# Up projection of a gated feed-forward block: eight half-size products per tile replaced by Strassen's seven, from the fourth tile on

## The reference

```
x = layer_norm(ALPHA * x + mix, ln1_g, ln1_b)            # 1024 prompt rows and 32 sample rows, 1024 columns
up = x @ ffn_w_up                                        # 1024 x 5632
u_conv, u_lin = up[..., :D_FF], up[..., D_FF:]           # D_FF = 2816
conv = sum(padded[:, j:j + T] * ffn_conv_w[j] for j in range(3)) + ffn_conv_b
h = silu(conv) * u_lin
x = layer_norm(ALPHA * x + h @ ffn_w_down, ln2_g, ln2_b)
```

## Time and profile before

| | |
|---|---|
| median of 3 runs | 1707.56 us |
| profiled execution | 1713.04 us, span 1711.3 us |
| TensorE busy over the span | 1600.2 us (94%) |
| VectorE, ScalarE, GpSimd busy | 929.2, 665.8, 337.5 us (54, 39, 20%) |
| rest of tile 0 to tile 21 of the up projection | 1002 to 1461 us |
| down projection | 1461 to 1703 us |
| granted TensorE clock | 1.00 from 897 us on, mean of the span 0.955 |

### The profile page before, as it was taken

How to read it: one execution, slowest core, us unless ns; L and a number is a source line. 1 busy time by engine, 2 the same in 40 slices (tenths; PEclk the granted TensorE clock), 3 DMA queues, 4 the chain that set the end, 5 groups by cost and what they waited for, 6 DMA issues and landing times.

```text
span 1711.3 us, 39992 instructions
## 1 busy us (share of the span) xinstructions
PE 1600.2 (94%) x17211; PEld 1160.9 (68%) x17211; DVE 929.2 (54%) x2152; ACT 665.8 (39%) x1145; POOL 337.5 (20%) x209
## 2 busy tenths in 40 slices
PE   6899999979899788988879999999999999999998
PEld 4486666645667566766658866666666666888887
DVE  3699999985767557777532954333333333000046
ACT  4733222114677545666463143333333333211110
POOL 3322111012210211121113022222222222111100
PEclk9999999988999788899889999999999999999999
DMA  8123121333511203010122212111111110511001
GB/s 298 47 75 125 51 92 52 101 134 118 180 53 29 60 18 111 23 41 3 53 112 79 112 65 75 50 50 50 50 50 50 50 50 30 200 50 51 26 26 77
DMA packets 50370, 126.85 MB, mean 74 GB/s; under 512 B 17426, under 2 KB 24338, under 8 KB 42354
## 3 DMA queue, kind: packets, MB, share of 16 engines
q1 hardware_dynamic: 49106, 123.23, 21.2%
q0 software_dynamic: 1088, 1.05, 0.2%
HBM read 100.49 MB, written 23.77 MB: 73 GB/s over the span
## 4 chain that ended last, share of the span: by engine, by line
PE 70%; DVE 21%; ACT 4%; issue 3%; SPq 2%; DMA 1%; DVEq 0%; ACTq 0%
PE bank L2294 66%; DVE arena L2698 12%; PE bank L2457 2%; DVE arena L2718 1%; PE bank L1031 1%; PE bank L976 1%; DVE arena L2734 1%; DVE arena L2658 1%; SPq L924 1%; DVE arena L2716 1%; DVE arena L2719 1%; ACT L1405 1%; DVE arena L1648 0%; DVE arena L2712 0%; PE bank L1911 0%
## 5 line engine op out<-in xcount | busy, mean ns | idle before, releaser
L2294 PE MATMUL bank<-arena 64*64 64x64 f32 (+11 forms) x16504 | 1515.9, 288 | 91.7 <-ACT arena L1378 17.7
L2294 PEld LDWEIGHTS bank<-arena 128*128 128x128 f16 (+7 forms) x16504 | 1083.5, 123 | 523.1 <-issue 133.3
L2810 POOL TENSOR_TENSOR arena<-arena 128x2048 f16<-128x2048 f32 x53 | 216.0, 4078 | 775.0 <-ACT arena L2500 762.5
L2698 DVE TENSOR_SCALAR_CACHE_REDUCE arena<-arena 128x384 bf16<-128x384 f32 (+6 forms) x231 | 196.9, 917 | 1.2
L2499 ACT ACTIVATE arena<-arena 128x2048 f16<-128x2048 f32 x53 | 100.7, 1901 | 167.2 <-PE bank L2294 144.0
L2098 DVE TENSOR_SCALAR arena<-arena 128x1072 f32<-128x1072 f32 x22 | 26.5, 1205 | 172.7 <-issue 165.6
L2516 ACT ACTIVATE arena<-bank 128x352 f32<-128x352 f32 x72 | 33.2, 463 | 189.0 <-PE bank L2294 189.0
L1782 POOL TENSOR_TENSOR arena<-arena 128x512 f32<-128x512 f32 x40 | 54.7, 1377 | 258.4 <-PE bank L2294 127.7
L2500 ACT ACTIVATE arena<-arena 128x2048 f32<-128x2048 f32 x53 | 100.5, 1896 | 0.0
L2110 DVE SCALAR_TENSOR_TENSOR arena<-bank,arena 128x352 f32<-128x352 f32 (+1 forms) x66 | 33.5, 513 | 111.3 <-PE bank L2294 84.5
L2837 POOL TENSOR_TENSOR arena<-arena 128x512 f32<-128x512 f32 (+1 forms) x32 | 38.5, 1206 | 199.6 <-DVE arena L2767 116.0
(11 more groups left out here) (265 smaller groups left out, 1137.7 us busy)
## 6 DMA issues: line engine op xcount, KB each, us to landing
arena<-slabs SPq DMA_DIRECT2D x53, 1024.0 KB, 5.0
arena<-kcache SPq DMA_DIRECT2D x32, 256.0 KB, 2.9
arena<-vcache SPq DMA_DIRECT2D x32, 256.0 KB, 3.1
prw<-arena SPq DMA_DIRECT2D x42, 176.0 KB, 1.9
arena<-xt SPq DMA_DIRECT2D x4, 1056.0 KB, 8.4
x1d<-arena SPq DMA_DIRECT2D x8, 512.0 KB, 2.6
arena<-x1d SPq DMA_DIRECT2D x1, 4096.0 KB, 13.1
y<-arena SPq DMA_DIRECT2D x8, 512.0 KB, 2.6
```

The lines of the kernel that those rows point to most:

```text
L2294: return nc.tensor.matmul(out, lhsT, rhs, start=start, stop=stop, skip_group_check=True)
L2698: last = dve.tensor_scalar(junk, a, s, None, op, ALU.add, accum_out=cnt[:, k:k + 1])
L2810: pool.tensor_tensor(WL[r].rearrange("p a b -> p (a b)"), STG[s], WH[r].rearrange("p a b -> p (a b)"), ALU.subtract).then_inc(slab_lo, 1)
```

## The change

Tiles 0 to 2 are computed as before. From tile 3 on (`UP_PLAIN` = 3) the product of a tile's weights and the activations is taken as a 2 x 2 block product: the weights in blocks (convolved or linear half; blocks 0 to 3 or 4 to 7 of the model columns), the activations in blocks (model columns; first or second half of the tokens, 528 each, `TH2`). The seven products of Strassen's method (in Winograd's form) are made instead of eight, each over 4 column blocks. `UP_PRODUCTS` gives their order, the bank pair of each and the moving operand. A product is two jobs of 12 matmuls of 264 columns (`TC`). The banks a, d and c take a first product, which ScalarE copies out, and then go on accumulating a second one on top; b takes one. Eight banks in all, a pair for each letter; a job waits for the same bank of the tile before.

- Token sums: VectorE makes T1, T2, T4 and GpSimd T3 (`TF`, sums and differences of quarters of XH and XL, 4 x 528 = 2112 elements a partition, five and three instructions), ScalarE writes their high parts (`TH`), VectorE three low parts and GpSimd one (`THL`). This is done once, in tiles 0 to 2.
- Weight sums, every tile from 3 on: ScalarE scales the slab (`up_scale`), VectorE makes four sums of 4 x 128 elements (`up_sums`), ScalarE writes 7 x 512 high parts in four instructions (`up_hi`) and GpSimd the low parts in four (`up_lo`).
- Results, every tile from 3 on: ScalarE copies six half banks into `UQ1`, `UQ7`, `UQ5` and the final a pair into `HF`. VectorE combines b, d and c with them, and builds the fourth block from SBUF alone. Convolution, SiLU, h and its two parts are as before, but h of tile f is made while tile f+1 runs, and its product is SBUF by SBUF.
- h of tiles 8 to 18 is written to DRAM (`hd`, 11 x 540 KB), each before a later slab is loaded, and read back when the up projection ends, into the place of the token sums and of `UQ`, `US`. TensorE waits for the reads before the second and third slab group of down (n = 0).
- The fourth weight slab of down is loaded after the up projection instead of in it; the conv output is stored later.

```
+UP_PRODUCTS = (("a", "x11"), ("d", "t3"), ("c", "t1"), ("b", "t2"), ("a", "x21"), ("d", "t4"), ("c", "x22"))
+UP_BANKS = (("b", "dve"), ("a", "act"), ("d", "dve"), ("c", "dve"))
...
+            def up_products(f):                      # TensorE
+                i = f - UP_PLAIN
+                wh, wl = UWH[f % 2], UWL[f % 2]
+                for c, (name, rhs) in enumerate(UP_PRODUCTS):
+                    xh, xl, k0, t0 = moving[rhs]
+                    if c in (0, 2, 4):
+                        pe.wait_ge(uw_lo, 3 * i + c // 2 + 1)
+                    if c == 6:
+                        pe.wait_ge(slab_lo, SL_UP + f + 1)
...
+                    for n in range(2):
+                        if c < 4:
+                            b = open_bank(pe, (name + "up", f, n))
+                        else:
+                            b = bank((name + "up", f, n))
+                            pe.wait_ge(part_read, 6 * i + 2 * (c - 4) + n + 1)
+                        s = slice(t0 + TC * n, t0 + TC * n + TC)
+                        for k in range(4):
+                            w = slice(up_weight(c, k), up_weight(c, k) + P)
+                            mm(b[:, 0:TC], wh[:, w], xh[:, k0 + k, s], c < 4 and k == 0, False)
+                            mm(b[:, 0:TC], wh[:, w], xl[:, k0 + k, s], False, False)
+                            last = mm(b[:, 0:TC], wl[:, w], xh[:, k0 + k, s], False, k == 3)
+                        last.then_inc(part_filled if c < 3 else filled, 1)
...
             for n in range(3):                       # down, TensorE
...
                     if n == 0:
                         pe.wait_ge(hl_ready, sum(DN_G[:g]) + kn)
+                        for q in ((), (0, 1), (2,))[g]:
+                            pe.wait_ge(h_in[q], 16)
...
+            for f in range(UP_PLAIN, FT):            # ScalarE
+                i = f - UP_PLAIN
+                if i:
+                    act.wait_ge(q_ready, 2 * i)
+                for k, (name, dst) in enumerate((("a", UQ1), ("d", UQ7), ("c", UQ5))):
+                    if i and k == 1:
+                        act.wait_ge(c22_ready, i)
+                    for n in range(2):
+                        act.wait_ge(part_filled, 6 * i + 2 * k + n + 1)
+                        act.activation(dst[:, TC * n:TC * n + TC], bank((name + "up", f, n))[:, 0:TC], ACT.Copy,
+                                       scale=UN).then_inc(part_read, 1)
+                if f + 2 < FT:
+                    up_scale(f + 2)
+                if i:
+                    up_silu(f - 1)
+                act.wait_ge(hl_ready, f - 1)
+                for n in range(2):
+                    b = wait_job(act, ("aup", f, n))
+                    act.activation(HF[:, f % 2, TC * n:TC * n + TC], b[:, 0:TC], ACT.Copy, scale=UN).then_inc(freed["act"], 1)
+                if i:
+                    up_hh(f - 1)
+                if f + 2 < FT:
+                    up_hi(f + 2)
...
             for f in range(UP_PLAIN):                # ScalarE, tiles 0 to 2; m = 0 banks, then:
+                if f == 0:
+                    token_hi(0)
+                    token_hi(1)
+                    token_hi(2)
+                if f == 2:
+                    token_hi(3)
...
+                up_silu(f)
                 act.activation(HH[f], HF[:, f % 2, :], ACT.Copy, scale=XS).then_inc(hh_ready, 1)
+                if f == 0:
+                    up_scale(UP_PLAIN)
+                if f == 1:
+                    up_hi(UP_PLAIN)
+                    up_scale(UP_PLAIN + 1)
+                if f == 2:
+                    up_hi(UP_PLAIN + 1)
...
+            token_sum(0, ...)                        # VectorE, ahead of tile 0: three instructions of 2112
+            token_sum(1, ...)                        # two
             for f in range(UP_PLAIN):                # VectorE, after conv, h and the low part of tile f:
+                if f == 0:
+                    token_lo(0, 0, 1)
+                    up_sums(UP_PLAIN)
+                if f == 1:
+                    token_lo(1, 1, 2)
+                    dve.wait_ge(t_lo, 2)
+                    token_sum(0, ...)                # two
+                    token_lo(3, 0, 3)
+                    up_sums(UP_PLAIN + 1)
...
+            for f in range(UP_PLAIN, FT):            # VectorE
+                i, u = f - UP_PLAIN, UPB[:, f % 2, :]
+                dve.wait_ge(cn_ready, f - 1)
+                dve.tensor_copy(sampled_up(u, 0, 2), SCV[:, f, :].rearrange("p (b x) -> p b x", x=2))
...
+                    b = wait_job(dve, ("bup", f, n))                         # twice
+                    dve.scalar_tensor_tensor(UQ[:, s], b[:, 0:TC], UN, UQ1[:, s], ALU.mult, ALU.add).then_inc(freed["dve"], 1)
...
+                link(dve.scalar_tensor_tensor(UQ5, UQ5, 1.0, UQ, ALU.mult, ALU.add))
+                dve.scalar_tensor_tensor(u[:, 2 + TH2:2 + T], UQ5[:, 0:pn], 1.0, UQ7[:, 0:pn], ALU.mult, ALU.add)
...
+                if i:
+                    up_h(f - 1)                                              # 1024 and 32 elements
+                if f + 2 < FT:
+                    up_sums(f + 2)                                           # four of 512
+                for n in range(2):
+                    b = wait_job(dve, ("dup", f, n))
...
+                if i:
+                    up_hl(f - 1)
+                for n in range(2):
+                    b = wait_job(dve, ("cup", f, n))
...
+                up_conv(f)
...
+            pool_link(pool.tensor_tensor(TF[2], quarter(XH, 1, 1), quarter(XH, 0, 1), ALU.subtract))   # GpSimd, once
+            pool_link(pool.tensor_tensor(TF[2], TF[2], quarter(XL, 1, 1), ALU.add))
+            pool.tensor_tensor(TF[2], TF[2], quarter(XL, 0, 1), ALU.subtract).then_inc(t3f_ready, 1)
+            def up_lo(f):
+                for g, (c0, c1) in enumerate(UP_GROUPS):                     # 1024, 1024, 1024, 512 elements
...
+                    pool.tensor_tensor(UWL[f % 2][:, s], up_source(f, g), UWH[f % 2][:, s],
+                                       ALU.subtract).then_inc(uw_lo if g < 3 else slab_lo, 1)
...
+                if f == 0:                                                   # GpSimd, per tile, after the CN copies
+                    pool.wait_ge(t3_hi, 1)
+                    pool.tensor_tensor(THL[2], TF[2], TH[2], ALU.subtract).then_inc(t3_lo, 1)
+                if 0 < f < FT - 2:
+                    up_lo(f + 2)
...
+            for w in range(SL_UP + 4, SL_DN + 3):                            # SyncE
+                f = w - SL_UP - 5
+                if 0 <= f - HKEEP < HSPILL:
+                    sp.wait_ge(hl_ready, f + 1)
+                    sp.dma_start(hd[f - HKEEP], arena[:, HB[f]:HB[f] + TOK]).then_inc(h_out, 16)
                 load_slab(w)
...
             sp.wait_ge(filled, plan.last_of_slab[SL_DN - 1] + 1)
+            sp.wait_ge(h_out, 16 * HSPILL)
+            reload(0, 0, 5, MX0)
+            load_slab(SL_DN + 3)
+            reload(1, 5, 3, MX0 + 5 * TOK)
+            sp.wait_ge(hl_ready, FT)
+            reload(2, 8, HSPILL - 8, UP0)
```

235 lines of the change are left out of this document (194 added, 41 removed).

## The result

| | before | after |
|---|---|---|
| median, of 4 runs each | 1708.14 us | 1686.14 us |
| lowest to highest | 1707.27 to 1714.22 | 1685.49 to 1691.91 |
| profiled execution, span | 1713.04, 1711.3 us | 1686.14, 1684.4 us |
| TensorE waits of tiles 0 to 4 | 0 | 22.99 us |
| TensorE's restart to the start of down | 458.34 us | 435.85 us |

The ratio is 0.9866, 95% interval 0.9845 to 0.9887: 22 us faster. Predicted were 17 us (1691): 49 us of TensorE's own time, less what the start of the new scheme, the lower clock after its waits and VectorE's loop in the steady state were to cost.

A forecast was written before the change was run, and what follows sets the result against it. TensorE alone was taken to bound both projections. 1713.0 (profiled execution) - 49.0 + 25.5 + 2.5 + 4 + 0 = 1696.0, less 5.5 to the median: 1690.5, said as 1691 us; range 1667 to 1714, the forecast's own 1681 to 1701.

The forecast's parts named there:

- TensorE's own time: 19 changed tiles of the up projection: each from 21.48 to 18.90 us, 49.0 us saved in all.
- Turns of VectorE and GpSimd: Changed tiles: VectorE instructions with two SBUF sources and GpSimd's block each other; 6.4 us a tile, less 0.15 to 0.2 for each of five.
- VectorE's loop, 19.1: Steady state: VectorE's loop of 19.1 us against TensorE's 18.9 sets the tile; 4 us of TensorE waiting over 17 tiles.
- Start of the scheme, 25.5: Tiles 0 to 3: token and weight sums make TensorE wait 4.8, 3.9 and 16.8 us, 25.5 us in sum.
- Lower clock after waits, 2.5: After TensorE's waits the granted clock stays lower for a while: 2.5 us lost, bounds 0 and 6.
- Start of down, 0: Start of down: split and read-back done at +17.5 us, hidden behind 21.7 us of TensorE work; cost 0.
- 5.5 us between the profiled execution and the median: Whole kernel: the median shown is 5.5 us below the profiled execution, so 1696.0 becomes 1690.5.
- A: Changed tiles: holding does not bite, pieces fall into VectorE's idle time, the start costs 8 us; 1667 us; chance 0.13.
- B: Changed tiles: held instructions save nothing of their own time, loop 20.4 us; about 1711 us; chance 0.17.
- C: Changed tiles: VectorE and GpSimd in series set the tile, 21.2 us; slower, 1726 us; chance 0.12.
- D: Start of down: waits for the read-back, 5 us and a clock fall of 2; 1698 us; chance within the forecast's 0.58.

The follow-up runs named there:

- the kernel with one more pass: Against the kernel after: a second convolution pass (two SBUF sources, 1072 columns) made twice on VectorE in each changed tile; stretch 439.40 us, median 1691.44 us.
- the kernel with half a last product: Against the kernel after: the seventh product of each changed tile over two of its four blocks; stretch 417.63 us, median 1666.04 us.

## Why the prediction was right, point by point

The costs against the 49 us were put at 32.0 us (25.5 + 2.5 + 4) and came to 26.5; this is nearly all of the 5 us by which the forecast was too slow. One thing was luck. The forecast had VectorE set the pace of the steady state, and TensorE sets it. The error in VectorE's loop, 0.9 us a tile, cost only the 4 us of that term, because below 18.9 us a shorter loop gives nothing more. With a loop of 20.0, as far off the other way, the steady state would have cost some 13 us (an estimate, 17 x 1.1 less the 5.4 of the banks' slack). This slack the sum left out: in the kernel with one more pass VectorE fell behind for 11 tiles by 0.49 us each, 5.4 us, before TensorE waited. So even a loop of 19.1, 17 x 0.2 = 3.4 us behind, would have cost nothing.

- **TensorE's own time.** Exact: 112.5 ns a matmul, 18.90 us a tile, 49.0 us in all. The eighth product put back cost 51.2 us against 51.3 by the same rate.
- **Turns of VectorE and GpSimd.** The mechanism held, and its size too. (The prediction speaks mostly of instructions with two SBUF sources; the first pass and the copy have one, and were held as well, 1.97 us for 0.86 and 1.13 for 0.17.) The passes and the copy take 1.97 + 3.08 + 3.08 + 1.13 = 9.26 us; alone they are 0.86 + 2 x 1.34 + 0.17 = 3.71. That is 5.5 us of holding a tile, where the prediction had 6.4 less five savings of 0.15 to 0.2. Without most of GpSimd's low parts 5.6 us a tile vanished from VectorE's busy time.
- **VectorE's loop, 19.1: too long by 0.9.** The mis-sized term is VectorE's work without holding, "13.8 with the self-waits, about 13.5 where instructions overlap". Measured: 18.2 less 5.5, so 12.7. In the rows below, from one start to the next, the sums of 528, 496 and 32 take 1.44 us instead of 1.7, h in two instructions 1.24 instead of 1.5, the four weight sums 2.90 instead of 3.0, two bank reads in a row 0.69 instead of 0.86. So the loop fits into 18.9 us, and the 4 us that were to be lost in the steady state were not. The prediction's margin was 0.2 us; the real one is 0.7 on the other side.

VectorE in the kernel after, between the rows shown above:

```profile
1218.23 0.71 DVE L2369 SCALAR_TENSOR_TENSOR arena<-arena 128x528 f32<-128x528 f32 x1
...
1219.67 1.22 DVE L2351 SCALAR_TENSOR_TENSOR arena<-arena 128x1024 f32<-128x1024 f32 x1
...
1220.91 0.70 DVE L2289 SCALAR_TENSOR_TENSOR arena<-arena 128x512 f32<-128x512 f32 x1
...
1223.81 0.77 DVE L2381 SCALAR_TENSOR_TENSOR arena<-bank,arena 128x264 f32<-128x264 f32 x2
1224.50 1.25 DVE L2305 SCALAR_TENSOR_TENSOR arena<-arena 128x1056 f16<-128x1056 f32 x1
1225.67 0.77 DVE L2388 SCALAR_TENSOR_TENSOR arena<-bank,arena 128x264 f32<-128x264 f32 x2
```

- **Start of the scheme, 25.5: 23.0.** VectorE's first convolution pass was expected 27.8 us after the restart and came after 27.6 (1025.32 - 997.70, the row below). Waits of 4.8, 3.9 and 16.8 us were expected; 4.35, 1.83 and 16.81 came. The mis-sized one is ScalarE's, the second, and the reason is the clock: after the first wait TensorE ran its 120 matmuls in 19.75 us instead of 17.9 and so met the late bank 1.8 us later. In the kernel with half a last product they took 20.46 us and the wait was 1.12: the sum, 21.58 us, is the same.

```profile
1025.32 0.84 DVE L2297 TENSOR_SCALAR arena<-arena 128x1072 f32<-128x1072 f32 x1
```

- **Lower clock after waits, 2.5: about 3.5.** From the stretch: 458.34 - 49.0 + 22.99 = 432.3, and 435.85 were measured. 1.8 us of it is this slow piece, which only replaces waiting, 1.5 the one behind the long wait (356.5 us to down for 3156 matmuls, 355.0 at 112.5 ns). Waits and clock together: 28.0 expected, 26.5 measured.
- **Start of down, 0.** Right. Down begins without a wait, and the read-back is hidden although the residual's read took 19.1 us instead of 13.1.

The chain: 1713.04 - 49.0 + 23.0 + 3.5 = 1690.5, and the profiled execution was 1686.1. The remaining 4.4 us are the earlier stages, which the change does not touch: TensorE's restart came at 997.70 against 1002.11. The prediction's 5.5 us between the profiled execution and the median stood for this.

The rivals. **A** (no holding, 1667) is refuted by the start, which cost 23 us and not 8, though in the steady state TensorE does pace, as A said. **B** (held instructions save nothing, loop of 20.4) is refuted by the loop of 18.2: even on the measured 12.7 us of work its 6.4 us of holding would make 19.1. The passes show the turn itself: a piece of 1024 elements (2.04, half of the 4.07 of the earlier trace rows) and a pass (1.34) follow each other every 3.11 us (1231.47 - 1228.36), where their lone times add up to 3.38. The section "A bandwidth-pool intuition that's wrong (but worth ruling out)" of the Trainium skill's page "SBUF — State Buffer" has what was blocked by the other engine's lock go on about 115 ns after that one's end; it measured this on GpSimd's descriptor writing behind a VectorE copy. An estimate by that figure makes the turn 2.04 + 0.12 + 1.34 = 3.5 us. The trace disagrees, by 0.4 us. **C** (slower) needed a loop of 20.1. **D** (a wait at the read-back) did not come.

Granted clock after the waits of the kernel after (columns as above; the clock is the third number from the end):

```profile
1034.00:1038.00 4.00, 3.56 (x16) 2.02 (x17) 2.85 (x6) 2.66 (x2) 0.00 (x0) 0.68 0.00 0
1077.00:1081.00 4.00, 3.96 (x24) 2.93 (x25) 2.85 (x5) 3.06 (x4) 0.95 (x1) 0.64 0.00 0
```

TensorE had stood 4.35 and 16.81 us before them. 0.68 and 0.64 are means between its two levels, 1.2 and 2.4 GHz; in 1120:1400 it is at 1.00.

What is open: the spread of the earlier stages, 994.1 to 1002.8 us at the restart over the profiled executions, was not looked into; it is larger than several of the differences studied here.

## What to carry to other kernels

When TensorE sets the time and a change takes matmuls away for work on other engines, add up the loop of the engine that gets the work with everything that holds it, and compare it with TensorE's new time per tile; here it was 18.2 against 18.9, and it fits only just. Price the one-off start separately: it took back 26.5 us of 49. Moving T4 within the same three tiles gave nothing: the waits got shorter and more, and the lower clock after each took the gain. One tile more of room (price 2.6 us), the token work on one engine and ScalarE's bank reads put first gave back 17 us. Elementwise work that was on GpSimd to relieve VectorE was not hidden here, where VectorE's queue was full; it cost VectorE GpSimd's longer time.

## What the runs showed of the hardware

- VectorE and GpSimd instructions with SBUF operands take turns, one of each, when both queues are full: a pair of 2.36 and 4.2 us takes 6.27 (1014.97 - 1008.70). A 16-column copy takes 1.13 us in place of 0.17 at such a place, and GpSimd's copy of two columns 1.11 beside VectorE's h.
- In such turns each pair takes 0.3 us less than its two lone times (3.11 for 3.38, 6.27 for 6.56; GpSimd's lone times, 2.04 and 4.2, are worked out by elements from 4.07 for 2048). The prediction had 0.15 to 0.2, from instructions of 512 elements.
- VectorE's busy time includes the time held: 94% busy in the stretch, and 5.6 of 17.8 us a tile of it standing.
- The lower clock after a wait can cost nothing where a late bank follows (19.75 + 1.83 and 20.46 + 1.12 us), and it can take a gain back: 2.6 us of waits less, in six pieces instead of three, left the stretch 0.6 us longer.
